# Issuing sixteen projection loads from the SyncE queue instead of the ScalarE queue in a two-layer hybrid decoder kernel

## The reference, cut to what matters

```python
for l in range(DEPTH):                     # DEPTH = 2
    h = _rmsnorm(x, w['norm_mix_g'][l])
    proj = jnp.einsum('bld,de->ble', h, w['w_in'][l])
    lru_x, lru_gate, r_q, r_k, r_v, r_g, s_z, s_xbc, s_dt = _split_cols(proj, IN_SIZES)
    xc, lru_buf = _causal_dwconv(lru_x, ...)          # width 4
    y_a = h_lru.astype(x.dtype) * jax.nn.gelu(lru_gate)
    ...                                               # retention
    xbc, ssd_buf = _causal_dwconv(s_xbc, ...)         # width 4, on four tiles of each SSD group
    xbc = jax.nn.silu(xbc)
    ...                                               # SSD scan, output projection
    x = x + jnp.einsum('blf,fd->bld', jax.nn.gelu(gate) * up, w['ffn_w_down'][l])
```

## Time and profile before

| | us |
|---|---|
| runs (3), median | 2988.82 (2986.44 to 2998.12) |
| the profiled execution, its own time | 2988.82 |
| its span, first to last instruction | 2987.0 |
| PE busy | 2849.1 (95% of the span) |
| DVE busy | 1635.5 (55%) |
| ACT busy | 582.8 (20%) |
| POOL busy | 1019.5 (34%) |
| share of the 16 DMA engines, SP's queue (q1) | 21.8% |
| the same, ACT's queue (q10) | 0.9% |

### The profile page before, as it was taken

How to read it: one execution, slowest core, us unless ns; L and a number is a source line. 1 busy time by engine, 2 the same in 40 slices (tenths; PEclk the granted TensorE clock), 3 DMA queues, 4 the chain that set the end, 5 groups by cost and what they waited for, 6 DMA issues and landing times.

```text
span 2987.0 us, 46924 instructions
## 1 busy us (share of the span) xinstructions
PE 2849.1 (95%) x18164; PEld 2786.1 (93%) x18164; DVE 1635.5 (55%) x2122; ACT 582.8 (20%) x887; POOL 1019.5 (34%) x444
## 2 busy tenths in 40 slices
PE   7999999989999999999799999998999999999995
PEld 6999899989999999999789998998899999999995
DVE  4657776366444444444636586754564444444446
ACT  3323231123100111111213331311221111110002
POOL 3433222213434434344333333222134344343340
PEclk9999999999999999999999999999899999999997
DMA  4324334321111111111122334244011111111111
GB/s 152 118 72 141 126 105 144 96 98 37 44 49 49 42 49 46 46 49 42 53 76 99 124 111 141 76 149 150 30 44 43 49 49 42 49 46 46 49 42 76
DMA packets 75816, 227.94 MB, mean 76 GB/s; under 512 B 18672, under 2 KB 19696, under 8 KB 74624
## 3 DMA queue, kind: packets, MB, share of 16 engines
q1 hardware_dynamic: 73376, 217.66, 21.8%
q10 hardware_dynamic: 2304, 8.46, 0.9%
HBM read 180.63 MB, written 45.96 MB: 76 GB/s over the span
## 4 chain that ended last, share of the span: by engine, by line
PE 85%; DVE 6%; issue 4%; DMA 2%; PEld 1%; ACT 1%; SPq 1%; POOL 1%; DVEq 0%; ACTq 0%; POOLq 0%; PEldq 0%
PE ps L649 26%; PE ps L651 25%; PE ps L650 25%; DVE sb_pt L1345 1%; DMA sb_ch<-sin 1%; PE ps L759 1%; PE ps L817 1%; PE ps L761 1%; SPq L446 1%; PE ps L880 1%; PE ps L764 0%; PE ps L881 0%; PE ps L738 0%; DVE sb_x L1820 0%; PE ps L782 0%
## 5 line engine op out<-in xcount | busy, mean ns | idle before, releaser
L649 PE MATMUL ps<-sb_h_hi,sb_w_hi 128*128 128x344 f32 x3744 | 1222.9, 327 | 27.1 <-POOL sb_w_lo L631 21.9
L650 PE MATMUL ps<-sb_h_lo,sb_w_hi 128*128 128x344 f32 x3744 | 1206.3, 322 | 0.0
L651 PE MATMUL ps<-sb_h_hi,sb_w_lo 128*128 128x344 f32 x3744 | 1205.9, 322 | 0.0
L628 POOL TENSOR_TENSOR sb_w_hi<-sb_w_raw,sb_ones 128x1024 fp32r<-128x1024 f32 x220 | 426.1, 1937 | 1892.7 <-PEq L646 940.1
L649 PEld LDWEIGHTS ps<-sb_h_hi,sb_w_hi 128*128 128x128 f32 x3744 | 713.9, 191 | 36.6 <-issue 32.3
L650 PEld LDWEIGHTS ps<-sb_h_lo,sb_w_hi 128*128 128x128 f32 x3744 | 713.9, 191 | 1.3
L651 PEld LDWEIGHTS ps<-sb_h_hi,sb_w_lo 128*128 128x128 f32 x3744 | 713.5, 191 | 0.0
L631 POOL TENSOR_TENSOR sb_w_lo<-sb_w_raw,sb_w_hi 128x1024 fp32r<-128x1024 f32 x220 | 593.3, 2697 | 17.2
L649 PE MATMUL ps<-sb_y_hi,sb_w_hi 128*128 128x344 f32 x1536 | 507.9, 331 | 45.9 <-DVE sb_x L1335 24.4
L651 PE MATMUL ps<-sb_y_hi,sb_w_lo 128*128 128x344 f32 x1536 | 499.4, 325 | 0.0
L650 PE MATMUL ps<-sb_y_lo,sb_w_hi 128*128 128x344 f32 x1536 | 496.4, 323 | 0.0
(11 more groups left out here) (243 smaller groups left out, 2201.2 us busy)
## 6 DMA issues: line engine op xcount, KB each, us to landing
sb_w_raw<-w SPq DMA_DIRECT2D x222, 512.0 KB, 3.5
proj<-sb_ev SPq DMA_DIRECT2D x64, 516.0 KB, 2.9
sb_pt<-proj SPq DMA_DIRECT2D x32, 516.0 KB, 4.9
sb_raw<-proj SPq DMA_DIRECT2D x16, 516.0 KB, 5.5
sb_raw<-proj ACTq DMA_DIRECT2D x16, 516.0 KB, 3.8
sb_ch<-cumT SPq DMA_DIRECT2D x32, 256.0 KB, 4.0
sb_x<-x SPq DMA_DIRECT2D x8, 516.0 KB, 8.1
sb_raw<-proj SPq DMA_DIRECT2D x32, 129.0 KB, 5.0
```

The costliest lines, as they stand in the source:

```text
L628: nc.gpsimd.tensor_tensor(w_hi[:, q, :], w_raw[:, q, :], ones[:, 0:1].to_broadcast([P, 1024]), ALU.mult).then_inc(sg.sem("w_hi_done"), 1)
L649: mm(o, wh, ah, start=first, stop=False)
L650: mm(o, wh, al, start=False, stop=False)
L651: return mm(o, wl, ah, start=False, stop=last)
```

## The change

The two ScalarE helpers are gone. SyncE issues the same sixteen loads: `load_lru_gates(u)` for units 0 and 1, and `load_conv(u, 2)` and `load_conv(u, 3)` at the head of `prep(u)` in units 2 and 3, each behind a wait of SyncE for `conv_done (u, 0)` or `(u, 1)`. The signals `raw_turn` and `lru_gate_loaded` become `raw_loaded` and `gate_loaded`. In units 2 and 3 ScalarE takes the tap of tile 2 ahead of the SiLU of tile 1. No data size and no arithmetic changes.

```diff
@@ def load_conv(u, j, tile)
                 stored(tile)
-                sp.dma_start(raw[:, j, 3:T + 3],
-                             io["proj"][tile]).then_inc(*sg.on("raw_loaded" + str(j), (u, j), 16))
+                if j >= 2:
+                    sp.wait_ge(*sg.after("conv_done", (u, j - 2)))
+                    step()
+                sp.dma_start(raw[:, j % 2, 3:T + 3],
+                             io["proj"][tile]).then_inc(*sg.on("raw_loaded" + str(j % 2), (u, j), 16))
...
+            def load_lru_gates(u):
+                t0 = TILE0[UNITS[u]]
+                for j in (2, 3):
+                    stored(t0 + j)
+                    sp.wait_ge(*sg.after("conv_done", (u, j - 2)))
+                    step()
+                    sp.dma_start(raw[:, j - 2, 0:T], io["proj"][t0 + j]).then_inc(*sg.on("gate_loaded", (u, j), 16))
...
             def prep(u):
+                t0 = TILE0[UNITS[u]]
+                if u < 2:
+                    load_lru_gates(u)
+                    return
+                if u < 4:
+                    for j in (2, 3):
+                        load_conv(u, j, t0 + j)
                 if u == 2:
...
                 if u < 2:
+                    if u == 0:
+                        prep(0)
                     for point, _ in POINTS[u]:
                         ended(PLAN[u][point])
                         if (u, point) == (1, "pre"):
+                            prep(1)
                             sp.wait_ge(*sg.after("cumT_ready"))
...
-        def load_s(u, j):
-            tile = TILE0[UNITS[u]] + j
-            act.wait_ge(*sg.after(f"ev_stored{EV[tile]}", tile))
-            act.wait_ge(*sg.after("conv_done", (u, j - 2)))
-            act.dma_start(raw[:, j - 2, 3:T + 3],
-                          io["proj"][tile]).then_inc(*sg.on(f"raw_turn{j - 2}", (u, j), 16))
...
@@ units 0 and 1, ScalarE
-                for j in (2, 3):
-                    load_gate(u, j)
...
-                act.wait_ge(*sg.after("lru_gate_loaded", (u, 3)))
+                act.wait_ge(*sg.after("gate_loaded", (u, 3)))
...
@@ units 2 and 3, ScalarE
-                load_s(u, 2)
                 silu(u, 0)
-                load_s(u, 3)
+                tap_s(u, 2)
                 silu(u, 1)
-                tap_s(u, 2)
                 tap_s(u, 3)
```

More of the change, by code:

```diff
@@ L1044, in y_free @@
                 act.wait_ge(*sg.after("p_ready", RING["out", u - 1, KD - 1, NG - 1]))
-        def load_s(u, j):
-            tile = TILE0[UNITS[u]] + j
-            act.wait_ge(*sg.after(f"ev_stored{EV[tile]}", tile))
-            act.wait_ge(*sg.after("conv_done", (u, j - 2)))
-            act.dma_start(raw[:, j - 2, 3:T + 3],
-                          io["proj"][tile]).then_inc(*sg.on(f"raw_turn{j - 2}", (u, j), 16))
-        def load_gate(u, j):
-            tile = TILE0[UNITS[u]] + j
-            act.wait_ge(*sg.after(f"ev_stored{EV[tile]}", tile))
-            act.wait_ge(*sg.after("conv_done", (u, j - 2)))
-            act.dma_start(raw[:, j - 2, 0:T], io["proj"][tile]).then_inc(*sg.on("lru_gate_loaded", (u, j), 16))
         def tap_s(u, j):
@@ L1061, in tap_s @@
             slot = j if j < 2 else X0[u] + j - 2
-            act.wait_ge(*sg.after(f"raw_loaded{j}" if j < 2 else f"raw_turn{j - 2}", (u, j)))
+            act.wait_ge(*sg.after(f"raw_loaded{j % 2}", (u, j)))
             if (u, j) == (2, 2):
```

## The result

The changed kernel takes 3008.64 us (median of 7 runs, 3005.29 to 3018.0); the kernel before, run beside it, 2988.82 (7 runs). The ratio is 1.0074, 95% interval 1.0057 to 1.0091: it is slower by 20 us, where 11.5 were forecast. On another chip the ratio was 1.0086 (1.0072 to 1.0101). The profiled execution took 3004.08 us, 15 more than the one of before and less than any of the seven.

What follows compares the result with a forecast made beforehand. TensorE was taken to bound the kernel (85% of the chain of waits). Late slot 19 weights (3.6 and 4.9 us) and low clock (1.5 per layer) summed to 11.5 on 2988.8, so 3000 us, range 2988 to 3009.

Steps and rivals of the forecast that it cites:

- Units 0 and 1: Units 0 and 1: SyncE's new waits fit into its idle time, so all eight gate loads cost 0.
- Slot 19 in layer 0: Unit 2, layer 0: weights for i8, queued behind SyncE's wait and 3.42 MB, come late; TensorE waits 3.6 us.
- Slot 19 in layer 1: Unit 2, layer 1: the same weights come 6.1 us late, of which 1.2 come back, leaving 4.9.
- The 1.2 us: Unit 2, layer 1: later TensorE waits of 0.7 and 0.5 us run out during the new wait.
- Low clock: Unit 2, both layers: TensorE's clock drops behind the new wait, 1.5 us each, bounds 0 and twice that.
- Both terms with what comes back: Unit 2, both layers: late weights (3.6 and 4.9) plus low clock (1.5 each), 11.5 us.
- Unit 3: Unit 3: slot 27's weights have 3 us left; one TensorE wait shrinks, another grows; 0, bounds -2.1 and +1.5 per layer.
- the sum: Whole kernel: 3.6 + 4.9 + 1.5 + 1.5 + 0 = 11.5 us, from units 2 and 3.
- The chances: Whole kernel: within 0.5% 0.74, slower by more 0.23, faster by more 0.03.
- The rival of 18.7 us: Slot 19, both layers: waits above 5 us, doubled low clock, no 1.2 back, low clock in unit 3; 3007, chance 0.20.
- its 3.0 us in unit 3: Unit 3, both layers: the grown wait is followed by a low clock stretch of its own, 1.5 us each.

Runs made afterwards that it cites:

- u2_only: Against the kernel before, only the two raw loads of unit 2 go to SyncE, the others stay on ScalarE; 3006.35 us, ratio 1.0070.
- after_split_late: Kernel after, but the weight load whose split GpSimd begins beside unit 4's rotation waits until the rotation is done; 2997.92 us, ratio 1.0047 against before.
- Padding: Five more SyncE semaphore increments ahead of unit 4: on the kernel before 2987.97 us; on the version with raw loads behind i6's (i12's) store and weight load 2991.99.

## Why the prediction was wrong: a right mechanism in unit 2, and no term for unit 4

- **Units 0 and 1, 0:** right (ratio 0.9998).
- **Slot 19 in layer 0, 3.6:** the landing was forecast for 270.0 and came at 271.0 (the stage began 0.95 later), the split took 4.9 for 4.8. TensorE was due at 271.18 and came at 270.1, since the earlier split of the earlier trace rows no longer held up VectorE ahead of it, so that the 1.83 us wait became 1.2, and since the clock stayed at 1.00 in 266 to 270, where before has 0.57. So the wait is 5.9, but against before the piece starts only 276.03 - 271.18 = 4.85 later. Without the 0.95 it is 3.9, and that is the number that compares with 3.6.
- **Slot 19 in layer 1, 4.9:** it landed at 1751.48 (GpSimd's timeline of the kernel after, below) where 1743.7 was forecast, and the layer began 7.9 us later: right to 0.1 us. The piece starts at 1755.93, 5.6 us late without those 7.9, where 6.1 were forecast. The 1.2 us did come back: the profile of after has neither of the two short waits of the earlier trace rows.

```profile
1751.48 1.89 POOL L649 TENSOR_TENSOR sb_w_hi<-sb_w_raw,sb_ones 128x1024 fp32r<-128x1024 f32 x1 [20.51 <-DMA sb_w_raw<-w]
1753.45 2.35 POOL L652 TENSOR_TENSOR sb_w_lo<-sb_w_raw,sb_w_hi 128x1024 fp32r<-128x1024 f32 x1
```

- **Low clock, 1.5 each:** 2.4 and 2.9 in the profile of after, 1.4 in u2_only: the size is at or above the forecast, within its bounds of 0 and 3.0.
- **Both terms with what comes back:** some 20 us behind the new wait the kernel after stands at 7.0 in layer 0, of which 0.95 are from ahead of unit 2, and at 14.6 in layer 1, of which 7.9 are: 6.1 and 6.7 us, 12.8 against 11.5 forecast. In the second profile of after it is 5.7 and 5.4. The same term in the medians, after_split_late, is 12.4. At the end of the unit the table has only 4.5 for layer 0, and that is luck: in 341 to 345 before's clock is 0.57 (17 matmuls in 4 us), and that of after at the same work, in 348 to 352, is 1.00 (27).
- **Unit 3, 0 (-2.1 to +1.5):** right: -0.3 and +0.4 in the first profile, +0.7 and -2.0 in the second. Slot 27 landed at 404.28, which is 399.0 plus the 4.9 us by which the convolution ahead of it came later, and 0.4; nobody waited for it. One wait shrank by 2.1 us and the other grew by 2.8.
- **The step that failed** is that the sum ends with unit 3: unit 4 is put at nothing without a reason being given; I had taken it as untouched, since no instruction there moves. It costs 3.1 to 4.9 us in each profile and layer (to the eviction at 520.88 and 1991.91), 6.4 and 8.4 in the two profiles, by VectorE's rotation losing a second turn to GpSimd's split. With the 12.8 and 11.1 of unit 2 that makes 19.2 and 19.5, about the 20 us of the median. Taking the split away from the rotation gives back 11.8 us of the median, more than that, as the turn that before has goes with it. The rows of before showed the place: the add of 2.81 us beside the split of 508.38, and a margin of 0.66 us in layer 0 and 0.97 in layer 1. They did not show that the rotation would come late by more than this margin. I had read such rows only where the change touches the queue.
- **The chances:** 0.74 stood on a difference under 0.5%, and 0.74% was measured, at least 0.57%. The range of 2988 to 3009 holds the 3008.64 by its last 0.4 us, through the rival below and not through the sum.
- **The rival of 18.7 us** came near the time mostly by luck. Its condition (a wait above 5 us in both layers) held, and the low clock of layer 1 came near the doubled one in one profile. But its 3.0 us in unit 3 did not come (-2.0 to +0.7 there), nor its 1.2 of layer 1, which did come back. What fills the gap is unit 4, which it does not have.

Open: why SyncE takes 1 us more for the first partial loads of unit 4 once raw loads are moved, and why the rotation starts late behind its tail. Padding did not move either predictably, and two stretches have the second without the first. So it is shown that the collision costs, and that it nearly always comes with the moved loads, but not what happens between the two.

## What to carry to other kernels

A load that is moved to another issuer carries its wait into that issuer's queue. Count what stands behind it, with its bytes, up to the first transfer that the busiest engine needs; one added wait, without any load moved, cost 13.6 us where the whole change costs 20. Then look beyond the edit: wherever GpSimd's work and a two-input instruction of VectorE start less than a microsecond apart, as in unit 4 here, a shift ahead of that place can change the order, and that has a price of its own. Read those margins before you call a stage untouched.

## What the runs showed of the hardware

- GpSimd's split (1.90 and 2.40 us alone) and VectorE's rotation instructions (1.23 alone) ran in turns in unit 4 of the kernel after: each ended 1.1 us (VectorE) or 2.2 us (GpSimd) behind the other's end. Margins that differ by less than 0.2 us (0.05 ahead, 0.12 behind) gave one turn or two, and 24.6 or 26.9 us for the stretch.
- The granted clock stood at 0.50 in the first stretch of work behind waits of 4.2, 5.5 and 5.9 us alike; 17 matmuls of 0.14 us were lost behind 4.2, 10 or 17 behind 5.9, and 21 behind 6.1. Behind the same wait of 1.8 us it was 0.57 in layer 0 of the kernel before and 1.00 in layer 1. Two executions of the kernel after had 1.00 and 0.53 at the same matmuls with the same waits, which made 4.6 us.
- The landing of a weight load behind seven other transfers followed from their bytes at the 324 and 296 GB/s of the earlier trace rows and 1.9 us, within 0.2 us in both layers once the later start of the stage is taken off.
